# The first weight tile in halves around x, the first norm factors alone, and the compression sums in rows

## Chip, cores and metric
One core of one Trainium2 chip runs the kernel. The metric is the time on the device in microseconds, the median of the runs; all inputs and outputs are float32.

## The reference, cut to what matters
Two layers of a mixer over 512 positions of width 1024, and a final norm. Each layer norms x, multiplies by a wide `w_in`, feeds four branches (short convolution, sparse attention, retention, pooling), merges them and runs a gated feed-forward block. The part of the attention branch that the change touches compresses keys and values over overlapping windows of 32 positions, 16 apart (31 windows):

```python
def compress(t, w1, w2):
    tb = t[:, blk] + cmp_pe[None, None, :, None, :]     # blk: 31 windows of 32 positions
    hid = jax.nn.gelu(jnp.einsum('bnlgd,lde->bnge', tb, w1))
    return jnp.einsum('bnge,ef->bngf', hid, w2)

def hybrid_layer(x, norm1_g, w_in, ...):
    h = rms_norm(x, norm1_g)
    z = h @ w_in
...
```

## The kernel before
Activations lie transposed, features on the 128 partitions and the 512 positions along the free axis: x is eight blocks [128, 512]. Every weight matrix is cut into groups of 128x1024 (512 KB) of eight 128x128 chunks, which pass through a ring of three slots. Every product is made in three matmuls of a split: weights and activations are each kept as a high part (rounded by a copy) and a low part (the rest), and `product` (L1205 to L1207) adds high x high, high x low and low x high. So a tile of 512 columns costs 24 matmuls for its eight chunks, and two accumulator banks, `acc[0]` and `acc[1]`, take turns.

The engines' work is written out by hand, each engine in its own order, tied by counting semaphores. SyncE issues the weight groups: group g + 3 may come once the low half of group g is made. ScalarE makes the high parts (`w_hi`), VectorE the low parts of the first groups and of x, GpSimd all later low parts (L437). `hi_ready` and `lo_ready` count them, `lo_ready` twice for each group, because low parts are made in halves of four chunks, and TensorE waits for the second half only in the middle of a tile (`second_half`). The factors of all norms, gate biases, taps and the position terms `pe` lie in one table, `vc_` [128, 294] (147 KB), and `norm1` is its first eight columns.

At the start SyncE issues group 0, the table, the eight blocks of x, group 1, the square part of the constants, group 2, the other constants, group 3 and on. ScalarE makes w_hi of group 0 and then xg_hi block by block (L511), VectorE w_lo of group 0 and then xg_lo (L712), and TensorE follows a block behind (`wait=1` of tile 0). Until then TensorE runs 14 products of zeros (L1200). After that ScalarE makes group 1, two squares of x, group 2, six squares, and enters the loop over the layers, where each step first makes the high part two groups ahead. Tile 2 uses `acc[0]` again and so waits for ScalarE's copy of tile 0, k_cmp (L527).

The first twelve tiles of a layer (`A_TILES`) are the keys and values of the compression, the other keys and values, the queries and the gates. VectorE scales k_cmp and v_cmp by the norm and then adds the position terms (`windows`, L795): the 512 positions are split into even and odd (on the partitions, q), sixteen-position groups m (32 of them) and places r in them (8); the result `win` [128, 2, 2, 256] keeps, for each of two term sets a and each key group g, 32 x 8 values. After tile 6 TensorE multiplies them (`compress`, L1298): 16 steps l, each for k and v, of 31 windows for two key groups, 62 columns, with weights of 64 columns. k goes to the lower 64 output partitions, v to the upper ones. In VectorE's order `take` (L732) empties tiles: take(4), win_v, two rotations, take(5), a copy, take(6), and then the sums of the compression. Tile 7 goes to the bank that take(5) empties.

Of the kernel before, what the change touches and what calls it, by code (L numbers as in the profile page):

```python
# [23 lines left out]
F32 = mybir.dt.float32  # L24
F32R = mybir.dt.float32r
ALU = mybir.AluOpType
ACT = mybir.ActivationFunctionType
AX = mybir.AxisListType

P = 128  # L30
S = 512
D = 1024
DC = D // P
# [5 lines left out]
HEADS, KV_GROUPS, DH = 8, 2, 64  # L39
BLOCK, STRIDE = 32, 16  # L40
NCMP = (S - BLOCK) // STRIDE + 1
# [7 lines left out]
CH = 8  # L49
# [9 lines left out]
GROUPS = D0 + DC * DG  # L59
# [123 lines left out]
def build(nc, xT, weights, vec, w1, pool_w, consts, decay, out):  # L183
    with ExitStack() as ctx:
        sem = lambda name: ctx.enter_context(nc.semaphore(name))
# [5 lines left out]
        def at(name, shape, dt, offset):  # L191
            n = 4 * int(np.prod(shape[1:]))
            assert base + offset + n <= nc.sbuf_usable_end, (name, offset)
            return nc.alloc_sbuf_tensor_at(name, shape, dt, offset=base + offset)
# [4 lines left out]
        w_raw = at("w_raw", [P, RING, CH * P], F32, 48 * KB)  # L199
        w_hi = at("w_hi", [P, RING, CH * P], F32R, 60 * KB)  # L200
        w_lo = at("w_lo", [P, RING, CH * P], F32R, 72 * KB)
# [49 lines left out]
        vc_ = at("vec", [P, NVEC], F32, R3)  # L251
# [21 lines left out]
        def V(name, i=0, n=1):  # L273
            return vc_[:, VEC[name] + i:VEC[name] + i + n]
# [11 lines left out]
        raw_ready = [sem(f"raw_ready{i}") for i in range(RING)]  # L286
        hi_ready = sem("hi_ready")
        lo_ready = sem("lo_ready")
# [9 lines left out]
        mean_ready = sem("mean_ready")  # L298
        spread_ready = sem("spread_ready")
        vec_ready = sem("vec_ready")  # L300
        w2v_ready = sem("w2v_ready")
        w1_ready = [sem("w1k_ready"), sem("w1v_ready")]
        x_in = [sem(f"x_in{c}") for c in range(DC)]
# [77 lines left out]
        @block.sync  # L381
        def _(sp):
            def load_group(g, slot):
                sp.dma_start(w_raw[:, slot, :],
                             weights[bass.ds(g, 1), :, :].rearrange("a p n -> (a p) n")).then_inc(raw_ready[slot], 16)

            def load_groups(L, first, last):

                with sp.Fori(0, (last - first) // RING) as t:
                    for k in range(RING):  # L390
                        g = L * GROUPS + t * RING + (first + k)
                        sp.wait_ge(lo_ready, 1 + 2 * (g - (RING - 1)))
                        load_group(g + 0, (first + k) % RING)

            load_group(0, 0)
            sp.dma_start(vc_[:, :], vec[0, :, :]).then_inc(vec_ready, 16)
            for c in range(DC):
                sp.dma_start(x[:, c, :], xT[:, c, :]).then_inc(x_in[c], 16)
            load_group(1, 1)
            squares = CON["causal"]  # L400
            sp.dma_start(con[:, 0:squares], consts[:, 0:squares]).then_inc(square_ready, 16)
            load_group(2, 2)
            sp.dma_start(con[:, squares:], consts[:, squares:]).then_inc(con_ready, 16)
            with sp.Fori(0, LAYERS) as L:


                sp.wait_ge(halves, 1 + L * (2 * GROUPS))
                for k in range(RING):
                    g = RING + k
                    sp.wait_ge(lo_ready, 1 + 2 * (L * GROUPS + (g - (RING - 1))))  # L410
                    load_group(L * GROUPS + g, g % RING)
                    if k == 2:
                        sp.dma_start(w2v[DH:P, :], vec[bass.ds(L, 1), 0:DH, VEC["w2v"]:VEC["w2v"] + DH].rearrange("a p n -> (a p) n")).then_inc(w2v_ready, 16)
                    if k < 2:
                        sp.dma_start((w1k, w1v)[k][:, :, :],
                                     w1[bass.ds(L * 2 + k, 1), :, :, :].rearrange("a p l n -> (a p) l n")).then_inc(w1_ready[k], 16)
                load_groups(L, 2 * RING, D0 + RING)

                sp.wait_ge(act_ready, 1 + L * FC + FC)
                sp.dma_start(vc_[:, :], vec[bass.ds(L + 1, 1), :, :].rearrange("a p n -> (a p) n")).then_inc(vec_ready, 16)  # L420


                load_groups(L, D0 + RING, GROUPS + RING)
            for c in range(DC):
                sp.wait_ge(y_ready, c + 1)
                sp.dma_start(out[:, c, :], x[:, c, :]).then_inc(stored, 16)
            sp.wait_ge(stored, 16 * DC)
# [20 lines left out]
        def _(act):  # L448
# [47 lines left out]
                    act.dma_start(dst[64:128, :], src[0:64, :]).then_inc(rot_ready[i % 2], 16)  # L496


            act.wait_ge(zero_made, 2)
            nc.scalar.activation(pad_out, pad_out, ACT.Sqrt)  # L500

            def first_high(g):

                act.wait_ge(raw_ready[g], 16)
                nc.scalar.activation(w_hi[:, g, :], w_raw[:, g, :], ACT.Copy).then_inc(hi_ready, 1)

            first_high(0)
            act.wait_ge(vec_ready, 16)
            for c in range(DC):
                act.wait_ge(x_in[c], 16)  # L510
                nc.scalar.activation(xg_hi[:, c, :], x[:, c, :], ACT.Copy, scale=V("norm1", c)).then_inc(x_hi_ready, 1)  # L511
            first_high(1)
            for c in range(DC):
                if c == 2:
# [145 lines left out]
        def _(dve):  # L660
            ve = nc.vector
# [35 lines left out]
                dve.sem_inc(s, 1)  # L697
            ve.memset(rstd[:, 0:P], 0.0).then_inc(zero_made, 1)
            ve.memset(small[:, :], 0.0).then_inc(zero_made, 1)
            dve.wait_ge(vec_ready, 16)  # L700
            def first_low(g):

                dve.wait_ge(hi_ready, g + 1)
                for half in range(2):
                    part = slice(half * CH * P // 2, (half + 1) * CH * P // 2)
                    ve.tensor_tensor(w_lo[:, g, part], w_raw[:, g, part], w_hi[:, g, part].bitcast(F32),
                                     ALU.subtract).then_inc(lo_ready, 1)

            first_low(0)
            for c in range(DC):  # L710
                dve.wait_ge(x_hi_ready, c + 1)
                ve.scalar_tensor_tensor(out=xg_lo[:, c, :], in0=x[:, c, :], scalar=V("norm1", c), in1=xg_hi[:, c, :].bitcast(F32),  # L712
                                        op0=ALU.mult, op1=ALU.subtract).then_inc(xg_ready, 1)
# [11 lines left out]
            with dve.Fori(0, LAYERS) as L:  # L725
# [61 lines left out]
                def windows(src, dst, name):  # L787


                    view = src.rearrange("p (m r q) -> p q m r", r=STRIDE // 2, q=2)  # L790
                    pe_ = V("pe", 0, BLOCK).rearrange("p (a r q) -> p q a r", a=2, q=2)
                    for g in range(KV_GROUPS):
                        rows = slice(DH * g, DH * g + DH)
                        for q in range(2):
                            ins = ve.tensor_tensor(  # L795
                                dst[DH * q:DH * q + DH, :, g, :].rearrange("p a (m r) -> p a m r", r=STRIDE // 2),
                                view[rows, q, :, :].unsqueeze(1).to_broadcast([DH, 2, S // STRIDE, STRIDE // 2]),
                                pe_[rows, q, :, :].unsqueeze(2).to_broadcast([DH, 2, S // STRIDE, STRIDE // 2]), ALU.add)
                            if (g, q) != (1, 1):
                                ins.then_inc(chain, 1)  # L800
                                then.n += 1
                    v_end(ins, name)
# [364 lines left out]
                with dve.Fori(0, DC // 2) as t:  # L1167
# [3 lines left out]
                    for k in range(2):  # L1171
                        c = t * 2 + k
# [21 lines left out]
        def _(pe):  # L1194
# [1 line left out]
            used = {"s": 0, "t": 0}  # L1196
            pe.sem_inc(halves, 1)
            pe.wait_ge(zero_made, 1)
            for _ in range(14):
                mm(acc[1][:, 0:P], rstd[:, 0:P], rstd[:, 0:P], start=True, stop=True)  # L1200

            def product(tile, slot, chunk, right_hi, right_lo, first, last):
# [6 lines left out]
            with pe.Fori(0, LAYERS) as L:  # L1209
                used.update(s=0, t=0)  # L1210

                def group_here(g, loop=None, per=0):

                    v = L * GROUPS + (g + 1)
                    if loop is not None:
                        v = v + loop * per
                    pe.wait_ge(hi_ready, v)
                    pe.wait_ge(lo_ready, 2 * v)

                def second_half(g, loop=None, per=0):  # L1220

                    v = L * GROUPS + (g + 1)
                    if loop is not None:
                        v = v + loop * per
                    pe.wait_ge(lo_ready, 1 + 2 * v)

                def tile_free(T, loop=None, per=0):
# [57 lines left out]
                def window(win, l):  # L1285

                    a, r = l // (STRIDE // 2), l % (STRIDE // 2)
                    return win[:, a, :, :].rearrange("p g (m r) -> p g m r", r=STRIDE // 2)[:, :, a:a + NCMP, r]

                def compress():  # L1290
                    for kind, i in (("k", 0), ("v", 1)):
# [185 lines left out]
                for b in range(B_GROUPS):  # L1477
                    g = A_GROUPS + b
# [9 lines left out]
                with pe.Fori(0, DC) as j:  # L1488
# [4 lines left out]
                    for n in range(4):  # L1493
                        g = J0 + 4 + n // 2
# [13 lines left out]
                for j in range(DC):  # L1508
                    g, T = O0 + j, TO0 + j
# [25 lines left out]
                with pe.Fori(0, DC // 2) as t:  # L1535
                    for k in range(2):
                        tile_free(TD0 + k, t, 2)
                        for c in range(FC):
                            g = D0 + DG * k + c // CH
# [143 lines left out]
```

## Time and profile before

| | us |
|---|---|
| median of 3 runs | 2072.21 |
| lowest, highest | 2071.92, 2073.07 |
| the profiled execution: own time | 2073.4 |
| its span | 2071.6 |
| busy: TensorE | 2043.5 |
| busy: VectorE, GpSimd, ScalarE | 1197.5, 917.5, 685.5 |

The page and the trace are of one execution, and its times are microseconds from the span's start. A timeline row gives start, duration, engine, line and operation, output <- inputs, and in brackets the idle time before it and what ended it. A row of the chain gives start, duration and what the end hung on. PE is TensorE's matmul, DVE VectorE, ACT ScalarE, POOL GpSimd, SPq the issuing of transfers on SyncE. A float32 matmul stands as two records, one for each pass. PEclk is the granted clock as a share of full.

### The profile page before, as it was taken

What the parts mean: (1) busy time and instruction counts of PE and PEld (TensorE: products, weight loads), DVE (VectorE), ACT (ScalarE), POOL (GpSimd) and SP (SyncE); (2) the same over time, 40 slices, a digit from 0 to 9 for tenths busy, and PEclk for the clock granted to TensorE, in tenths of its full rate; (3) what the DMA queues carried; (4) which work ended last, traced back from release to release, by engine and by line L of the source; (5) the groups of instructions that cost most, each with busy time, mean ns of one, the idle gap of its engine ahead of it and who ended that gap; (6) DMA issues with size and microseconds to landing.
All of it is one profiled execution on the core that took longest, in us unless ns stands there. A gap on an engine that the chain in (4) does not pass through costs nothing.

```text
span 2071.6 us, 32027 instructions
## 1 busy us (share of the span) xinstructions
PE 2043.5 (99%) x9840; PEld 1639.5 (79%) x9840; DVE 1197.5 (58%) x1799; ACT 685.5 (33%) x1011; POOL 917.5 (44%) x672
## 2 busy tenths in 40 slices
PE   8999999999999999999999999999999999999997
PEld 7777677888888888888887777778888888888886
DVE  7766865422327788862258677572322378888522
ACT  5355533323332322222233554333323232222222
POOL 4432233544445554545544212334444445555552
PEclk9999999999999999999999999999999999999998
DMA  5311122232232223223233112222323223222333
GB/s 210 107 52 52 62 89 90 91 96 96 91 101 96 92 97 101 91 94 112 95 125 95 56 49 66 92 91 92 101 91 101 91 92 102 91 101 95 101 105 108
DMA packets 57433, 194.91 MB, mean 94 GB/s; under 512 B 7040, under 2 KB 7552, under 8 KB 57216
## 3 DMA queue, kind: packets, MB, share of 16 engines
q1 hardware_dynamic: 52576, 186.17, 26.9%
q10 hardware_dynamic: 4768, 7.61, 1.4%
q8 instruction: 50, 0.82, 0.2%
q14 instruction: 39, 0.32, 0.1%
HBM read 186.67 MB, written 2.10 MB: 91 GB/s over the span
## 4 chain that ended last, share of the span: by engine, by line
PE 95%; DVE 3%; issue 1%; ACT 0%; DMA 0%; SPq 0%; DVEq 0%; ACTq 0%
PE acc L1205 29%; PE acc L1207 28%; PE acc L1206 28%; PE o L1416 2%; PE s L1390 2%; PE t L1398 1%; PE o L1455 1%; PE s L1445 1%; PE t L1436 0%; PE s L1298 0%; DMA w_raw<-weights_dram 0%; PE s L1471 0%; PE s L1462 0%; DVE ssq L1104 0%; DVE x L1189 0%
## 5 line engine op out<-in xcount | busy, mean ns | idle before, releaser
L437 POOL TENSOR_TENSOR w_lo<-w_raw,w_hi 128x512 fp32r<-128x512 f32 x668 | 917.3, 1395 | 1130.1 <-ACT w_hi L459 1114.2
L1205 PE MATMUL acc<-xg_hi,w_hi 128*128 128x512 f32 x1904 | 768.8, 404 | 5.8 <-DVE xg_lo L712 1.8
L1207 PE MATMUL acc<-xg_hi,w_lo 128*128 128x512 f32 x1904 | 743.0, 390 | 0.0
L1206 PE MATMUL acc<-xg_lo,w_hi 128*128 128x512 f32 x1904 | 741.9, 390 | 0.0
L459 ACT ACTIVATE w_hi<-w_raw 128x1024 fp32r<-128x1024 f32 x336 | 355.0, 1056 | 772.3 <-PE acc L1207 737.4
L1205 PEld LDWEIGHTS acc<-xg_hi,w_hi 128*128 128x128 f32 x1904 | 357.5, 188 | 115.3 <-issue 29.5
L1206 PEld LDWEIGHTS acc<-xg_lo,w_hi 128*128 128x128 f32 x1904 | 357.8, 188 | 76.1 <-issue 5.8
L1207 PEld LDWEIGHTS acc<-xg_hi,w_lo 128*128 128x128 f32 x1904 | 357.4, 188 | 76.2
L1082 DVE TENSOR_TENSOR work<-acc,rstd 128x512 f32<-128x512 f32 x64 | 44.1, 690 | 256.1 <-PE acc L1207 256.1
L1205 PE MATMUL acc<-act_hi,w_hi 128*128 128x512 f32 x352 | 136.9, 389 | 0.0
L1206 PE MATMUL acc<-act_lo,w_hi 128*128 128x512 f32 x352 | 136.9, 389 | 0.0
L1207 PE MATMUL acc<-act_hi,w_lo 128*128 128x512 f32 x352 | 136.9, 389 | 0.0
L1088 DVE SCALAR_TENSOR_TENSOR work<-work,acc 128x512 f32<-128x512 f32 x64 | 44.0, 688 | 103.1 <-PE acc L1207 103.1
L1176 DVE SCALAR_TENSOR_TENSOR x<-acc,x 128x512 f32 x16 | 11.1, 693 | 158.1 <-PE acc L1207 158.1
L1205 PE MATMUL acc<-y_hi,w_hi 128*128 128x512 f32 x256 | 99.6, 389 | 0.0
L1206 PE MATMUL acc<-y_lo,w_hi 128*128 128x512 f32 x256 | 99.6, 389 | 0.0
L1207 PE MATMUL acc<-y_hi,w_lo 128*128 128x512 f32 x256 | 99.6, 389 | 0.0
L635 ACT ACTIVATE work<-work 128x512 f32<-128x512 f32 x44 | 27.8, 632 | 192.2 <-DVE work L1131 192.2
L940 DVE COPY pT<-t 128x128 f32<-128x128 f32 (+3 forms) x128 | 56.7, 484 | 56.3 <-PE o L1416 56.0
L1207 PEld LDWEIGHTS acc<-act_hi,w_lo 128*128 128x128 f32 x352 | 66.1, 188 | 13.8
L1205 PEld LDWEIGHTS acc<-act_hi,w_hi 128*128 128x128 f32 x352 | 66.1, 188 | 13.8
L1206 PEld LDWEIGHTS acc<-act_lo,w_hi 128*128 128x128 f32 x352 | 66.1, 188 | 13.6
(211 smaller groups left out, 2230.0 us busy)
## 6 DMA issues: line engine op xcount, KB each, us to landing
w_raw<-weights_dram SPq DMA_DIRECT2D x339, 512.0 KB, 3.3
x<-xT_dram SPq DMA_DIRECT2D x8, 256.0 KB, 5.9
rot<-rq ACTq DMA_DIRECT2D x16, 128.0 KB
rot<-rk ACTq DMA_DIRECT2D x16, 128.0 KB
dec<-decay_dram ACTq DMA_DIRECT2D x8, 256.0 KB, 3.2
out_dram<-x SPq DMA_DIRECT2D x8, 256.0 KB, 2.7
con<-consts_dram SPq DMA_DIRECT2D x1, 1406.0 KB, 10.5
w1k<-w_dram SPq DMA_DIRECT2D x2, 512.0 KB, 8.9
```

The costliest lines, as they stand in the source:

```text
L437: nc.gpsimd.tensor_tensor(w_lo[:, slot, part], w_raw[:, slot, part], w_hi[:, slot, part].bitcast(F32), ALU.subtract).then_inc(lo_ready, 1)
L459: nc.scalar.activation(w_hi[:, slot, :], w_raw[:, slot, :], ACT.Copy).then_inc(hi_ready, 1)
L635: nc.scalar.activation(work[:, 2, :], work[:, 1, :], ACT.Tanh, scale=0.5).then_inc(silu_ready, 1)
L940: t_end(ve.tensor_copy(pT[:, u % 2, 0:w], t_of(e)[:, 0:w]), e)
L1082: ve.tensor_tensor(work[:, n, :], acc[n % 2][:, :], rstd[:, :], ALU.mult).then_inc(acc_free, 1)
L1088: ve.scalar_tensor_tensor(out=work[:, n, :], in0=work[:, n, :], scalar=1.0, in1=acc[n % 2][:, :], op0=ALU.add, op1=ALU.mult).then_inc(acc_ ...
L1205: mm(tile, w_h, right_hi, start=first, stop=False)
L1206: mm(tile, w_h, right_lo, start=False, stop=False)
L1207: return mm(tile, w_l, right_hi, start=False, stop=last)
L1390: mm(b[:, 0:w], qT[r, h % 4, qi * P:(qi + 1) * P], kT[r, br, 0:w], start=True, stop=True).then_inc(s_done, 1)
L1398: ins = nc.tensor.transpose(b[:, k * P:(k + 1) * P], pr_of(u)[:, k * P:(k + 1) * P], ident)
L1416: ins = mm(o_bank[qi % 2][d, j * P:(j + 1) * P], v[:, d], p[:, half, :], start=(br == 0 and k == 0), stop=(br == 1 and k == qi + 1))
```

## The change
The first weight group is loaded in two halves: the first ahead of x, the second between blocks 1 and 2 of x, and ScalarE and VectorE make its high and low parts in the same two halves. The eight columns of `norm1` are loaded alone, on ScalarE's queue; the rest of the table comes behind group 1. TensorE waits for the second half of w_hi in the middle of tile 0. The zero products go from 14 to 9. And `win` is stored with r outside and m inside, so that VectorE writes with a step of 32 elements and TensorE reads 31 neighbours for each key group.

```diff
@@ SyncE
-            load_group(0, 0)
-            sp.dma_start(vc_[:, :], vec[0, :, :]).then_inc(vec_ready, 16)
+            middle = CH * P // 2
+            sp.dma_start(w_raw[:, 0, 0:middle], weights[0, :, 0:middle]).then_inc(first_raw, 16)
             for c in range(DC):
                 sp.dma_start(x[:, c, :], xT[:, c, :]).then_inc(x_in[c], 16)
+                if c == 1:
+                    sp.dma_start(w_raw[:, 0, middle:], weights[0, :, middle:]).then_inc(raw_ready[0], 16)
             load_group(1, 1)
+            sp.dma_start(vc_[:, DC:], vec[0, :, DC:]).then_inc(vec_ready, 16)
@@ ScalarE
+            act.dma_start(vc_[:, 0:DC], vec[0, :, 0:DC]).then_inc(gain_ready, 16)
             act.wait_ge(zero_made, 2)
...
-            first_high(0)
-            act.wait_ge(vec_ready, 16)
+            act.wait_ge(first_raw, 16)
+            nc.scalar.activation(w_hi[:, 0, 0:middle], w_raw[:, 0, 0:middle], ACT.Copy).then_inc(first_hi, 1)
+            act.wait_ge(gain_ready, 16)
             for c in range(DC):
                 act.wait_ge(x_in[c], 16)
                 nc.scalar.activation(xg_hi[:, c, :], x[:, c, :], ACT.Copy, scale=V("norm1", c)).then_inc(x_hi_ready, 1)
+                if c == 1:
+                    act.wait_ge(raw_ready[0], 16)
+                    nc.scalar.activation(w_hi[:, 0, middle:], w_raw[:, 0, middle:], ACT.Copy).then_inc(hi_ready, 1)
@@ VectorE
-            dve.wait_ge(vec_ready, 16)
+            dve.wait_ge(gain_ready, 16)
...
-            first_low(0)
+            dve.wait_ge(first_hi, 1)
+            ve.tensor_tensor(w_lo[:, 0, 0:middle], w_raw[:, 0, 0:middle], w_hi[:, 0, 0:middle].bitcast(F32), ALU.subtract).then_inc(lo_ready, 1)
             for c in range(DC):
+                if c == 2:
+                    dve.wait_ge(hi_ready, 1)
+                    ve.tensor_tensor(w_lo[:, 0, middle:], w_raw[:, 0, middle:], w_hi[:, 0, middle:].bitcast(F32), ALU.subtract).then_inc(lo_ready, 1)
                 dve.wait_ge(x_hi_ready, c + 1)
@@ VectorE, windows
-                                dst[DH * q:DH * q + DH, :, g, :].rearrange("p a (m r) -> p a m r", r=STRIDE // 2),
+                                dst[DH * q:DH * q + DH, :, g, :].rearrange("p a (r m) -> p a m r", r=STRIDE // 2),
@@ TensorE
-            for _ in range(14):
+            for _ in range(9):
                 mm(acc[1][:, 0:P], rstd[:, 0:P], rstd[:, 0:P], start=True, stop=True)
...
+                    if g == 0 and loop is None:
+                        pe.wait_ge(first_hi, 1)
+                        pe.wait_ge(lo_ready, 2 * (L * GROUPS + 1))
+                        return
...
+                    if g == 0 and loop is None:
+                        pe.wait_ge(hi_ready, v)
                     pe.wait_ge(lo_ready, 1 + 2 * v)
...
-                    return win[:, a, :, :].rearrange("p g (m r) -> p g m r", r=STRIDE // 2)[:, :, a:a + NCMP, r]
+                    return win[:, a, :, :].rearrange("p g (r m) -> p g r m", r=STRIDE // 2)[:, :, r, a:a + NCMP]
```

## Rows read from the trace of the kernel before

**Rows 1.** The page's part 4, shares of the chain by engine.
```profile
PE 95%; DVE 3%; issue 1%; ACT 0%; DMA 0%; SPq 0%; DVEq 0%; ACTq 0%
```

**Rows 2.** Timeline of the head, ScalarE and TensorE.
```profile
6.83 5.49 ACT L511 ACTIVATE xg_hi<-x,vec 128x512 fp32r<-128x512 f32 x8 [1.62 <-DMA x<-xT_dram]
...
8.39 0.50 PE L1205 MATMUL acc<-xg_hi,w_hi 128*128 128x512 f32 x1 [1.76 <-DVE xg_lo L712]
...
19.23 1.28 ACT L459 ACT_TABLE_LOAD   x1
...
22.21 0.47 PE L1205 MATMUL acc<-xg_hi,w_hi 128*128 128x512 f32 x1 [1.57 <-ACT k_cmp L527]
```

**Rows 3.** Chain of waits in the head: start, duration, what.
```profile
5.68 7.34 DMA w_raw<-weights_dram
...
15.05 1.03 ACT w_hi L505
16.08 3.13 ACT first_sq L516 x6
```

**Rows 4.** Chain of waits, small products: squares, compression, vc, values.
```profile
27.91 0.79 PE s L1274 x8
...
51.57 3.80 PE s L1298 x64
...
67.19 0.36 PE s L1337 x16
...
179.34 1.02 PE o L1416 x16
...
226.39 1.24 PE o L1416 x20
```

**Rows 5.** Instructions of two lines: duration in ns, min/median/max.
```profile
L1298 PE MATMUL s<-win_k,w1k x64: 292/294/305, 51.5 to 1077.8; 128*64 128x62 f32 x64
...
L1416 PE MATMUL o<-pT,v_nat x8: 272/273/323, 158.2 to 158.5; 128*64 128x128 f32 x8
```

**Rows 6.** Timeline around the compression, layer 0 and layer 1.
```profile
41.71 4.92 DVE L795 TENSOR_TENSOR win_v<-v_cmp,vec 64x512 f32<-64x512 f32 x4
...
52.73 0.68 DVE L732 TENSOR_TENSOR sc<-acc,rstd 128x512 f32<-128x512 f32 x1
...
55.30 0.50 PE L1205 MATMUL acc<-xg_hi,w_hi 128*128 128x512 f32 x1
...
61.10 0.69 DVE L732 TENSOR_TENSOR qT<-acc,rstd 128x512 f32<-128x512 f32 x1 [4.41 <-PE acc L1207]
...
1075.32 0.68 DVE L732 TENSOR_TENSOR sc<-acc,rstd 128x512 f32<-128x512 f32 x1
...
1078.02 0.50 PE L1205 MATMUL acc<-xg_hi,w_hi 128*128 128x512 f32 x1
```

**Rows 7.** Instructions of line 795 that write win_k, both layers.
```profile
L795 DVE TENSOR_TENSOR win_k<-k_cmp,vec x8: 739/749/755, 33.5 to 1058.6; 64x512 f32<-64x512 f32 x8
```

**Rows 8.** Issues of x, groups 2 and 3 (timeline), their landing times (last column).
```profile
1.68 3.96 SPq L398 DMA_DIRECT2D x<-xT_dram  x8
...
7.06 0.64 SPq L384 DMA_DIRECT2D w_raw<-weights_dram  x1
...
8.76 0.35 SPq L384 DMA_DIRECT2D w_raw<-weights_dram  x1
...
x<-xT_dram SPq DMA_DIRECT2D x1, 256.0 KB, 5.1
...
w_raw<-weights_dram SPq DMA_DIRECT2D x1, 512.0 KB, 7.7
...
w_raw<-weights_dram SPq DMA_DIRECT2D x1, 512.0 KB, 10.7
```

**Rows 9.** TensorE in two stretches: us, busy (records), granted clock, DMA share, GB/s.
```profile
1.71:4.91 3.20, 3.20 (x15) 1.00 0.92 278
4.91:6.63 1.72, 1.72 (x15) 1.00 0.91 292
```

More of the change, by code:

```diff
@@ L300, in build @@
         vec_ready = sem("vec_ready")
+        gain_ready = sem("gain_ready")
+        first_raw = sem("first_raw")
+        first_hi = sem("first_hi")
         w2v_ready = sem("w2v_ready")
@@ L505, in first_high @@
                 nc.scalar.activation(w_hi[:, g, :], w_raw[:, g, :], ACT.Copy).then_inc(hi_ready, 1)
-            first_high(0)
-            act.wait_ge(vec_ready, 16)
+            middle = CH * P // 2
+            act.wait_ge(first_raw, 16)
+            nc.scalar.activation(w_hi[:, 0, 0:middle], w_raw[:, 0, 0:middle], ACT.Copy).then_inc(first_hi, 1)
+            act.wait_ge(gain_ready, 16)
             for c in range(DC):
@@ L707, in first_low @@
                                      ALU.subtract).then_inc(lo_ready, 1)
-            first_low(0)
+            middle = CH * P // 2
+            dve.wait_ge(first_hi, 1)
+            ve.tensor_tensor(w_lo[:, 0, 0:middle], w_raw[:, 0, 0:middle], w_hi[:, 0, 0:middle].bitcast(F32), ALU.subtract).then_inc(lo_ready, 1)
             for c in range(DC):
+                if c == 2:
+                    dve.wait_ge(hi_ready, 1)
+                    ve.tensor_tensor(w_lo[:, 0, middle:], w_raw[:, 0, middle:], w_hi[:, 0, middle:].bitcast(F32), ALU.subtract).then_inc(lo_ready, 1)
                 dve.wait_ge(x_hi_ready, c + 1)
```

## The prediction
> **What bounds the kernel now.** I read the page first. The chain that ended last runs 95% over TensorE's matmuls [rows 1]. So a microsecond is only worth something where TensorE itself does less, or where it stands still and what it waits for comes sooner. The change touches two such places: the first 22 us, and the block of compression products (L1298), which stands once in each layer.
>
> For the head I followed the chain of waits backwards from where TensorE last stands still. Tile 0 of the projections begins at 8.39, after 1.76 us of waiting for xg_lo; but TensorE stands again before tile 2, 1.57 us until 22.21, for the ScalarE copy of k_cmp [rows 2]. Everything gained before 22.21 that doesn't move that copy is given back there. The chain to it is ScalarE's: group 1 lands at 13.02, its high half follows, group 2's high half starts at 15.05, six squares end at 19.21, a table load of 1.28 us, w_hi, k_cmp [rows 2, 3]. The reader is to see that ScalarE, not TensorE, is the clock of the first 22 us.
>
> For the compression products: 64 records take 3.80 us in the chain. k and v go to different halves of the columns and start together, so this is 32 rounds of 0.119 us with the edges, for 62 columns [rows 4]. The values products load weights of the same shape (128x64, two halves) and stream 128 columns: their runs of 16 and 20 records take 1.02 and 1.24 us, so two rounds cost 0.22, one 0.11, or 0.86 ns a column. At that rate 62 columns are 0.053 us. That the rounds here take twice this, and that one matmul of 62 columns lasts 294 ns where one of 128 lasts 273 [rows 5], needs a reason. The visible difference is the moving operand: L1298 reads with a step of 8 elements (32 bytes), the values products read neighbours.
>
> **The change, part by part.** *Rows instead of interleaved sums.* L795 writes win as (r m) instead of (m r), and L1298 reads runs of 31 neighbours. Counts and shapes stay. If the step is the reason, a round falls from about 0.115 to 0.055: 32 x 0.060 = 1.9 us less in each layer. Two things could hold it up. Weight loads: eight records with 128-wide loads and one moving column take 0.79 us, 0.1 each [rows 4]; two 64-wide loads one after the other would also be 0.1, and nothing would be won. Against that stand the vc products, 16 records with 31-wide loads in 0.36 us, where loads in series would need 16 x 0.024 = 0.39 before any edge [rows 4]; and the values rounds hide both loads. So loads into different column halves overlap, and I take 0.055 to 0.06 a round; the bounds are 0.055 and no gain.
>
> What is late next: tile 7 needs acc[1], which VectorE frees with take(5). That ends at 53.41 while tile 7 starts at 55.30; in layer 1 at 1076.00 against 1078.02 [rows 6]. So at most 1.89 and 2.02 us can be taken, less a few hundredths for the signal. The gain just fits under this cap. take(7) follows a VectorE pause of 4.41 us [rows 6], so VectorE can follow from there on. I take 1.75 us a layer, 3.5 for both.
>
> VectorE's side: win_k's instructions last 749 ns each [rows 7], win_v's four in layer 0 take 4.92 us [rows 6] while GpSimd works on weights; an ordinary 512-column one lasts 0.68 to 0.69 [rows 6]. The write step goes from 4 to 128 bytes; the trace has no VectorE write with such a step. Lower bound nothing: the engine takes about 1.4 ns an element here, against TensorE's 0.86 a column, so it has more time for each access. Upper bound: what TensorE pays for its step. A matmul of 62 neighbours should last 273 less 66 columns of 0.86, 216 ns; 294 is 78 more, 1.3 ns a column. On 512 elements that is 0.65 us an instruction, 5.2 us for eight. It is nearest to L795 itself, whose reads already step over every second element and cost 0.06 us more than ordinary; I take 0 to 0.1 us for the eight together. If it is more, take(5) comes later by that much and every bit over the slack lands on tile 7. win_v is written at 41.71 + 4.92 = 46.63 [rows 6] and L1298 begins at 51.57 [rows 4], so the products themselves wait for it hardly even at the upper bound.
>
> *The head.* Before x0 SyncE now issues half of group 0 (256 KB) instead of all of it and the vector table (512 + 147 KB). x0 was issued at 1.68 and landed 5.1 later, at 6.78 [rows 8]; from there to group 1's landing at 13.02 [rows 3] came seven blocks and a group, 2304 KB, 370 KB/us. With 403 KB less ahead of it x0 comes up to 1.09 us sooner, near 5.7, and tile 0 begins near 7.3. But the second half of group 0 now stands between x1 and x2, so x2 to x7 gain only the table's 147 KB, 0.40 us. On ScalarE the second half of w_hi goes between x1 and x2 as well. ScalarE took 5.49 us for eight blocks [rows 2]; it has the lead of x0 to fit 0.6 us in. VectorE's w_lo of that half fits the same way. Group 1 is issued at the same place in SyncE's list (ten DMAs before it both times) and lands 0.40 sooner, 12.62. Group 2 now has the rest of the table ahead of it: the same bytes before it as before, so it lands at 7.06 + 7.7 = 14.76 as it did [rows 8], and its high half can't start before 14.8 instead of 15.05. So only 0.24 us of the head gets through: squares to 18.97, table load to 20.3, and group 3, landed at 8.76 + 10.7 = 19.46 [rows 8], doesn't stop w_hi. The moved part of the table and the constants behind it are issued some 0.5 us later; the cover is the full queue (7 to 10 us from issue to landing [rows 8]), and the table's first reader, VectorE's half_b, stands behind the eight sums of squares. The new small DMA (eight floats a partition) goes out on ScalarE's queue ahead of the table load; one of SyncE's issues takes 0.5 us (3.96 for eight [rows 8]), its landing has some three microseconds until x0's, and ScalarE would stand idle for w_raw anyway. If an issue there took longer than that idle time, only tile 0 would see it. Bounds for the head: 0.4 if group 2 lands earlier too, and 0.3 more if the queue starts more evenly; on the other side the 128 small packets and the later issues could take back the 0.24 and 0.2 more. I take 0.24.
>
> *Nine warm-up products for fourteen.* Records come at 0.213 us in the first 3.20 us (15 of them) and at 0.115 in the next 1.72 (15), while the granted clock column says 1.00 in both [rows 9]: TensorE goes from the pace of 1.2 GHz to that of 2.4 at 4.9. 18 records end near 5.3, long before x0; five products taken off cost nothing on the path. What they do to the clock is a rival.
>
> Sum: 3.5 + 0.24 = 3.74. The profiled execution had a span of 2071.6 and its own time 2073.4, 1.8 around the span that the change doesn't touch: 2067.9 and 2069.7. That execution stood 1.2 above the median 2072.21, so I forecast 2068.5. A measurement of this kernel can tell about 0.2%, 4.1 us, from no change: the forecast is a real gain that lies just inside.
>
> **The rivals.**
> *VectorE pays for the scattered writes* (other side). Place: the eight L795. With S the extra time of a layer's eight, tile 7 waits for take(5), so it starts S - 1.95 later than before (the mean slack of the two layers), whatever the products save. The kernel is slower by over 0.2% from 2(S - 1.95) - 0.24 = 4.1 on, S = 4.1, 0.5 us an instruction. At the upper bound, S = 5.2, it is 2 x 3.25 - 0.24 = 6.3 slower: 2078.5. For it: TensorE's rate for a step. Against: VectorE needs over 1.3 ns an element anyway. By the Trainium skill (SBUF — State Buffer, the section on the DMA port swizzle) SBUF has lines of 16 bytes, and each access that goes on to a new line pays: that would make TensorE's reads cheap and every write of L795 dear. By that rule this case is the likelier; the trace agrees for the read, and has no row for the write. Chance 0.07.
> *A small write price*, 0.1 to 0.3 us each, S = 0.8 to 2.4: take(5) becomes the limit and a layer gains 1.95 - S, 1.15 to -0.45: with the head 2069.7 to 2072.9. Chance 0.17.
> *The compression products don't get faster* (loads or issue bound them): only the head, 2072.0. Chance 0.13.
> *The clock stays low*: 18 warm-up records end within half a microsecond of the rise, and a pause of 2 us follows. If tile 0 starts at 1.2 GHz, three microseconds of products at half pace cost 1.6; TensorE has 1.57 + 0.24 of idle time before tile 2, so it is hidden and the time is the forecast's. It costs only if it lasts into tile 2. Chance of a visible loss 0.03: about 2070.
> *Forecast*: 0.60, own range 2067.4 to 2069.4; about four tenths of it lies under 2068.07, if the head gives more.
>
> **Numbers.** Faster by over 0.2%: 0.27, from the forecast alone. Slower: 0.07 and a little of the small price, 0.08. Within: 0.65. The range 2067.3 to 2072.2 takes in the forecast, the small price and the case without gain.
>
> **What would show it.** In the profile after: the L1298 chain piece near 1.9 us instead of 3.80, its matmuls near 215 ns; L795 still near 749; tile 7 of layer 0 near 53.5 and started by TensorE's own order or by VectorE's take; xg_hi at 5.8; group 1's high half at 12.7, group 2's at 14.8; tile 2 at 22.0. Wrong would be: L795 over 0.85 us, a TensorE wait for VectorE before tile 7, a round that stays over 0.1, or a tile 2 that starts at 22.2 or later.

## The result, and the profile after

The changed kernel takes 2081.49 us (median of 6 runs, 2079.61 to 2083.28), the kernel before 2072.8 beside it (6 runs, 2071.92 to 2073.07). The ratio is 1.0044, with a 95% interval of 1.0033 to 1.0056: the change makes the kernel slower, by 8.7 us. The prediction said 2068.5 with a range up to 2072.2, and gave 0.08 to slower: it was wrong, and its first rival was right in place and sign.

The page of the kernel after, its span and the chain that ended last by engine (line numbers of the kernel after are 17 to 23 higher around here: L795 is now L812, L732 is L749, L1205 is L1222, L1298 is L1321):

```profile
span 2079.6 us, 32010 instructions
...
PE 93%; DVE 5%; issue 1%; ACT 0%; DMA 0%; DVEq 0%; SPq 0%; ACTq 0%
```

VectorE's part of the chain has grown from 3% [rows 1] to 5%. Where it sits the instructions of the two changed lines show, with minimum, median and maximum in ns; they answer to [rows 5, 7]:

```profile
L812 DVE TENSOR_TENSOR win_k<-k_cmp,vec x8: 1099/1109/1992, 34.3 to 1064.4; 64x512 f32<-64x512 f32 x8
L812 DVE TENSOR_TENSOR win_v<-v_cmp,vec x8: 1095/1119/1289, 44.9 to 1075.1; 64x512 f32<-64x512 f32 x8
...
L1321 PE MATMUL s<-win_k,w1k x64: 222/222/268, 52.3 to 1080.8; 128*64 128x62 f32 x64
```

Both sides of the bet are here. TensorE's matmul of 62 columns falls from 294 to 222 ns, as forecast. VectorE's sum goes from 749 to some 1100 ns, which was forecast to cost nearly nothing. TensorE's list of waits has this as its first row (total, times, longest):

```profile
PE acc L1222 <- DVE sc L749: 9.6, 4, 4.2
```

Before, two such waits held 1.5 us together. The new ones stand in front of tile 7, once in each layer. VectorE's timeline of that stretch in layer 0 (start, us, line, operation):

```profile
33.60 0.69 DVE L848 TENSOR_TENSOR k_cmp<-k_cmp,rstd 128x512 f32<-128x512 f32 x1 [2.02 <-DVEq L786]
34.32 5.40 DVE L812 TENSOR_TENSOR win_k<-k_cmp,vec 64x512 f32<-64x512 f32 x4
...
44.86 4.73 DVE L812 TENSOR_TENSOR win_v<-v_cmp,vec 64x512 f32<-64x512 f32 x4
49.63 0.69 DVE L794 TENSOR_TENSOR rot<-rot,con 128x512 f32<-128x512 f32 x1
50.24 1.78 DVE L796 TENSOR_TENSOR kT<-kT,con 128x512 f32<-128x512 f32 x1
52.05 1.66 DVE L798 TENSOR_TENSOR kT<-kT,rot 128x512 f32<-128x512 f32 x1
53.63 1.77 DVE L794 TENSOR_TENSOR rot<-rot,con 128x512 f32<-128x512 f32 x1
55.33 1.74 DVE L796 TENSOR_TENSOR kT<-kT,con 128x512 f32<-128x512 f32 x1
57.11 0.69 DVE L798 TENSOR_TENSOR kT<-kT,rot 128x512 f32<-128x512 f32 x1
57.72 0.68 DVE L749 TENSOR_TENSOR sc<-acc,rstd 128x512 f32<-128x512 f32 x1
```

take(5) is the last row. It starts at 57.72 and not at 52.73 [rows 6], 4.99 later, of which 0.79 came in with the head (win_k starts at 34.32, [rows 6, 7] put it at 33.5). The other 4.2 us arise in this stretch: win_k 5.40 instead of four of 0.75 with their gaps, 2.3 longer, and the rotations 2.0 longer, though nothing in them was changed: four of the six take 1.7 us instead of 0.69, where before it were two. Those of 1.7 us run beside GpSimd's subtractions. GpSimd's timeline of the same time, after:

```profile
49.83 3.33 POOL L443 TENSOR_TENSOR w_lo<-w_raw,w_hi 128x512 fp32r<-128x512 f32 x2 [4.67 <-ACT w_hi L465]
53.59 2.94 POOL L443 TENSOR_TENSOR w_lo<-w_raw,w_hi 128x512 fp32r<-128x512 f32 x2 [0.43 <-ACT w_hi L465]
```

and before, where the two rotations that started inside the first of these rows (48.62 and 50.30) took 1.76 and 1.78:

```profile
48.02 3.52 POOL L437 TENSOR_TENSOR w_lo<-w_raw,w_hi 128x512 fp32r<-128x512 f32 x2 [3.57 <-ACT w_hi L459]
52.82 2.53 POOL L437 TENSOR_TENSOR w_lo<-w_raw,w_hi 128x512 fp32r<-128x512 f32 x2 [1.28 <-ACT w_hi L459]
```

On TensorE's side, the timeline and the stretches (busy us and count of PE, PEld, DVE, ACT and POOL, then PEclk, DMA share, GB/s):

```profile
58.55 0.70 PE L1222 MATMUL acc<-xg_hi,w_hi 128*128 128x512 f32 x1 [4.20 <-DVE sc L749]
```

```profile
54.00:58.50 4.50, 0.36 (x13) 0.22 (x8) 4.37 (x4) 0.00 (x0) 2.53 (x2) 1.00 0.54 168
58.50:60.00 1.50, 1.45 (x4) 1.19 (x5) 1.44 (x3) 0.00 (x0) 0.00 (x0) 0.54 0.48 194
60.00:62.00 2.00, 2.00 (x6) 1.55 (x5) 0.93 (x5) 0.00 (x0) 0.00 (x0) 0.50 0.08 14
62.00:64.00 2.00, 2.00 (x10) 1.63 (x9) 0.00 (x0) 1.33 (x2) 0.00 (x0) 0.99 0.10 18
```

TensorE ends the compression at 54.35 and stands until 58.55. Then the granted clock is 0.54 and 0.50, 1.2 GHz, until 62. The chain of waits shows what that costs:

```profile
59.68 0.43 PE acc L1224
60.10 0.43 PE acc L1222
...
62.44 0.23 PE acc L1222
```

A matmul takes 0.43 us of the chain and later 0.23. The nine that start from 58.55 on need 3.7 us, where nine at full clock need 2.1: another 1.6 us. Layer 1 repeats all of it: the stretch is 4.07 longer there (take(5) from 1075.32 to 1084.07, with win_k starting 4.68 later), TensorE waits 3.90, and behind the wait some four matmuls still start 0.23 to 0.30 apart, then eight 0.43 apart: the clock takes 1.6 us again.

The head, on ScalarE's timeline, against [rows 2, 3]:

```profile
3.58 0.63 ACT L516 ACTIVATE w_hi<-w_raw 128x512 fp32r<-128x512 f32 x1 [0.89 <-DMA w_raw<-weights_dram]
5.14 0.72 ACT L520 ACTIVATE xg_hi<-x,vec 128x512 fp32r<-128x512 f32 x1 [0.94 <-DMA x<-xT_dram]
...
13.60 1.06 ACT L512 ACTIVATE w_hi<-w_raw 128x1024 fp32r<-128x1024 f32 x1 [0.61 <-DMA w_raw<-weights_dram]
...
15.81 1.06 ACT L512 ACTIVATE w_hi<-w_raw 128x1024 fp32r<-128x1024 f32 x1
...
22.27 0.58 ACT L539 ACTIVATE k_cmp<-acc 128x512 f32<-128x512 f32 x1
```

ScalarE begins the first block 1.7 us sooner, but group 1 is 0.56 later, group 2's high half 0.76 later, and tile 2 starts at 22.99 instead of 22.21. The span by stages: tile 2 +0.8, cmp_keys of layer 0 (86.06 to 90.87) +4.8, end of layer 0 (677.41 to 682.45) +5.0, end +8.0.

### The profile page after: what moved, and what is told of

Its sections match the earlier page's. It is cut to its first block, busy times and chain, and to the rows that moved or that the text cites. A ratio compares the mean times of both kernels' runs of the same rounds, so it can differ in the third digit from the quotient of the medians.

```text
span 2079.6 us, 32010 instructions
## 1 busy us (share of the span) xinstructions
PE 2045.4 (98%) x9830; PEld 1639.0 (79%) x9830; DVE 1202.0 (58%) x1799; ACT 686.0 (33%) x1012; POOL 919.4 (44%) x672
## 4 chain that ended last, share of the span: by engine, by line
PE 93%; DVE 5%; issue 1%; ACT 0%; DMA 0%; DVEq 0%; SPq 0%; ACTq 0%
PE acc L1222 28%; PE acc L1224 28%; PE acc L1223 28%; PE o L1439 2%; PE s L1413 2%; PE t L1421 1%; PE o L1478 1%; PE s L1468 1%; PE t L1459 0%; DVE win_k L812 0%; PE s L1494 0%; PE s L1485 0%; DVE sc L749 0%; DVE kT L796 0%; DMA w_raw<-weights_dram 0%
## 5 line engine op out<-in xcount | busy, mean ns | idle before, releaser
L1222 PE MATMUL acc<-xg_hi,w_hi 128*128 128x512 f32 x1904 | 771.5, 405 | 11.8 <-DVE sc L749 9.6
L1222 PEld LDWEIGHTS acc<-xg_hi,w_hi 128*128 128x128 f32 x1904 | 358.9, 189 | 122.1 <-issue 36.6
L1222 PE MATMUL acc<-act_hi,w_hi 128*128 128x512 f32 x352 | 136.9, 389 | 0.0
L1222 PE MATMUL acc<-y_hi,w_hi 128*128 128x512 f32 x256 | 99.6, 389 | 0.0
L1222 PEld LDWEIGHTS acc<-act_hi,w_hi 128*128 128x128 f32 x352 | 66.1, 188 | 13.8
```

Of the source, the lines that this page charges most:

```text
L1222: mm(tile, w_h, right_hi, start=first, stop=False)
```

## Experiments

The theory is that the layout costs the time through VectorE: its writes with a step of 128 bytes make take(5) late, and TensorE's pause for it costs the clock as well. The rivals are the head, the products, and other causes of VectorE's lateness; each expectation names its own theories. All ratios are against the kernel before on the same chip, with 95% intervals; the edits are against the kernel before unless said otherwise.

**The layout alone.**

```
-   dst[...].rearrange("p a (m r) -> p a m r", r=STRIDE // 2),
+   dst[...].rearrange("p a (r m) -> p a m r", r=STRIDE // 2),
...
-   return win[...].rearrange("p g (m r) -> p g m r", r=STRIDE // 2)[:, :, a:a + NCMP, r]
+   return win[...].rearrange("p g (r m) -> p g r m", r=STRIDE // 2)[:, :, r, a:a + NCMP]
```

> Only the layout of win is changed (VectorE writes with a step of 128 bytes, TensorE reads neighbours); the head is that of before. Theory (late take): VectorE's window sums of 1.1 instead of 0.75 us put take(5) some 4 us later, TensorE waits about 4 us before tile 7 in each layer and runs at half pace for some 3 us behind the wait. The head's part was +0.8, so this gives 2072.8 + 7.2 = 2080, with L1298 at 1.96 us. Rival (the head and its transfers are the cause): 2069 to 2070, no long wait before tile 7.

Measured: 2083.13 us (2081.29 to 2083.67), ratio 1.0049 (1.0035 to 1.0063). Its waits of TensorE:

```profile
PE acc L1205 <- DVE sc L732: 9.6, 4, 4.2
```

The same row as in the kernel after. The whole loss is in the layout.

**The head alone** (all of the change but those two lines).

> Only the head is changed (halves of group 0, norm1 alone, nine warm-up products); win is laid out as before. Theory: tile 2 starts 0.8 us later, as in the changed kernel's profile, nothing else: 2073.6. Rival (the head is the cause): about 2080. My forecast for the head, 0.24 faster, would give 2072.6.

Measured: 2073.27 (2072.48 to 2075.03), ratio 1.0003 (0.9994 to 1.0012). The time can't be told from the kernel before; k_cmp starts at 22.13 in its trace, against 21.48 before. But over the ten traces of this study with the head of before it runs from 21.48 to 22.23, with a median of 21.78, and over the three with the new head from 21.89 to 22.27, with a median of 22.13. The trace of before was the earliest of its ten, and only some 0.35 us can be the head's.

**The read alone, and the write alone.** The first has only the second pair of lines above, the second only the first pair; both leave the sums in another order than their reader takes them.

> TensorE reads win as rows, VectorE still writes it interleaved as before, so the compression is computed from wrongly ordered sums; the work of both engines is otherwise that of before. Theory (the step of 32 bytes is what slowed the reads, VectorE's write step is what costs): 1.84 us less in each layer with take(5) just in time, 2069.2. Rival (the shorter products are no gain on the path, or need the new write): 2072.8.

> VectorE writes win as rows, TensorE reads it by the old step of 32 bytes, so the compression is computed from wrongly ordered sums; the work of both engines is otherwise the same. The products take 3.80 us again, so TensorE pauses about 2.3 us before tile 7 instead of 4.2. Theory: take(5) sets tile 7's start, the same as with the layout alone; if the shorter pause leaves the clock up, 2078, which would make the shorter products not only useless but the cause of the fall of the clock; if the clock falls all the same, 2081 to 2083. Rival (VectorE's price comes from both engines using rows at once, not from the write): VectorE back at 0.75 us a sum and 2072.8.

Measured: the read alone 2069.49 (2068.61 to 2070.13), ratio 0.9984 (0.9975 to 0.9993); the write alone 2079.75 (2078.93 to 2083.08), ratio 1.0038 (1.0024 to 1.0052). From the chain of the first, and one line's instructions:

```profile
51.88 2.01 PE s L1298 x64
```

```profile
L795 DVE TENSOR_TENSOR win_k<-k_cmp,vec x8: 737/750/759, 33.9 to 1056.7; 64x512 f32<-64x512 f32 x8
```

The second's:

```profile
L795 DVE TENSOR_TENSOR win_k<-k_cmp,vec x8: 1099/1110/1993, 34.3 to 1062.6; 64x512 f32<-64x512 f32 x8
```

```profile
PE acc L1205 <- DVE sc L732: 5.9, 4, 2.2
```

So the forecast's gain exists: 3.80 us of products become 2.01, twice, and 3.4 us come off the time with nothing lost. And the writes alone, with the products as slow as before, cost 6.9. Together they don't add to 3.5 but to 10.2 with the layout alone. The products that end 1.8 us sooner gain nothing there, since tile 7 waits for VectorE; they only lengthen TensorE's pause, from 2.2 to 4.2 us. In the write alone's trace the clock stays at full after layer 0's pause of 2.2 us, and falls after layer 1's.

**The layout with nine filler products behind the compression**, which keep TensorE busy until take(5) is nearly there.

```
+   for _ in range(9):
+       mm(o_bank[0][0:DH, 0:256], w1k[:, 0, :], win_k[:, 0, 0, :], start=True, stop=True)
```

> The layout alone, and behind the compression products nine more float32 products of 256 columns (3.9 us, into a bank that nobody reads then) that keep TensorE busy while VectorE comes to take(5). They change no result. Tile 7 starts as late as before the addition. Theory (part of the loss is the clock, which falls in the pause): the granted clock stays 1.00 and only the delay of tile 7 is left, 2.5 us a layer: 2078. Rival (the half pace behind tile 7's start has another reason): 2081 to 2083 as with the layout alone.

Measured: 2078.34 (2077.39 to 2078.92), ratio 1.0026 (1.0016 to 1.0035). Its stretches:

```profile
54.00:58.00 4.00, 3.71 (x18) 2.07 (x17) 3.85 (x4) 0.00 (x0) 2.01 (x2) 1.00 0.52 179
58.00:60.00 2.00, 1.97 (x9) 1.67 (x10) 1.90 (x5) 0.00 (x0) 0.00 (x0) 1.00 0.37 139
```

Tile 7 starts at 58.03, as late as with the layout alone (58.09), yet at full clock, and the kernel is 4.8 us shorter (3.9 between the two spans). Work that computes nothing makes it faster. The rows say the same: in the trace of the layout alone the slow matmuls cost 1.6 us behind layer 0's pause and 2.6 behind layer 1's, against the same tiles here. So the clock's share is shown: some 4 to 5 us of the 10 with the layout alone, 3.2 in the trace of the kernel after.

**take(5) ahead of the rotations**, in the kernel after, and with the layout alone.

```
                 windows(v_cmp[:, :], win_v, "win_v")
+                take(5, sc[:, 1, :])
...
-                take(5, sc[:, 1, :])
```

> The changed kernel with one line moved: VectorE does take(5) right behind win_v, before the two rotations, so that tile 7's bank is free about 7 us sooner. Theory: no wait before tile 7, no fall of the clock, and the whole 1.85 us of the shorter products in each layer counts: 2072.8 + 0.8 - 3.7 = 2070. Rival (slow window sums hold something else up too, so the wait only moves to a later tile): 2076 or more.

> The layout alone with take(5) moved ahead of the two rotations. The slow scattered sums stay. Theory: 3.6 us faster than before, 2069.2, TensorE's next wait for VectorE is the one before tile 12 as always. Rival (the sums delay more than take(5)): 2073 or more.

Measured: 2071.26 (2070.64 to 2074.74), ratio 0.9996 (0.9987 to 1.0005), and 2071.97 (2070.98 to 2073.11), ratio 0.9996 (0.9987 to 1.0005). One moved line takes back the 10 us of the kernel after:

```profile
49.25 0.69 DVE L749 TENSOR_TENSOR sc<-acc,rstd 128x512 f32<-128x512 f32 x1
```

take(5) is done before the compression ends at 54, and only the two old waits of 0.8 are left of that row. But the full gain of 3.4 doesn't come: with the layout alone it is 0.9. A new wait shows in both traces, 0.8 us in the first, and in the second:

```profile
PE s L1344 <- DVE kc L855: 1.3, 1, 1.3
```

VectorE is as late as before; it only owes its time to someone else. Against the read alone, TensorE gets past these products (L1344) 1.65 us later in layer 0 and 0.43 in layer 1: that is 2.1 of the 2.5 us that are missing.

**Neighbours in the write, a step of 64 bytes in VectorE's read.**

```
-   view = src.rearrange("p (m r q) -> p q m r", r=STRIDE // 2, q=2)
+   view = src.rearrange("p (m r q) -> p q r m", r=STRIDE // 2, q=2)
...
```

The output and the position terms are walked in the same new order, and TensorE reads neighbours.

> The same rows in win, made the other way round: VectorE goes through r outside and m inside, so that it writes neighbours and reads k_cmp and v_cmp with a step of 64 bytes. Theory A (only the scattered write costs): sums of 0.75 us, take(5) in time, 2069.3, faster than before. Theory B (every access to a new 16-byte line costs, read or write): 1.1 us or more and 2081 to 2083.

Measured: 2075.38 (2073.22 to 2077.1), ratio 1.0011 (1.0002 to 1.002).

```profile
L795 DVE TENSOR_TENSOR win_k<-k_cmp,vec x8: 1021/1038/1898, 33.8 to 1061.5; 64x512 f32<-64x512 f32 x8
```

1038 ns against 1109: VectorE pays for a read with a step too. The time fits neither theory of the run, 2.5 us above before: take(5) starts at 55.19, earlier than the 57.26 of the layout alone, and TensorE pauses 2.13 and 2.16 us instead of 4.20 and 3.90. The clock falls behind both pauses.

**The order changed once, in the products before.** k and v are multiplied by rstd in one instruction each, ahead of the eight sums. These two write their result in rows (sc[:, 2] and sc[:, 3]), and the sums read and write neighbours.

```
+   def to_rows(dst, src):
+       old = lambda t: t.rearrange("p (m r q) -> p m r q", r=STRIDE // 2, q=2)
+       return ve.tensor_tensor(dst.rearrange("p (q r m) -> p m r q", q=2, r=STRIDE // 2),
+                               old(src), old(rstd[:, :]), ALU.mult)
...
+   then(to_rows(sc[:, 2, :], k_cmp[:, :]))
+   windows(sc[:, 2, :], win_k, "win_k")
...
```

> The head of before. The rows are made once, in VectorE's two products by rstd (L831, L833), which now write k_cmp and v_cmp sorted by parity, place and group into free buffers; the eight window sums then read and write neighbours. Theory (a price per scattered instruction of about 0.35 us, paid twice instead of eight times): products of 1.0 to 1.1 us, sums back under 0.75, take(5) at most 0.4 us later than before, no pause over 0.3 us before tile 7, 2069.6. Rival (512 scattered elements on 128 partitions cost more, or the sums are slow for their four-dimensional pattern and not for the step): sums stay at 1.0 or more and 2075 to 2080.

> The same with take(5) ahead of the two rotations. Theory: nothing is left to wait for before tile 7 and VectorE is not behind later either: 2069.2, within 0.5 us of the one without the move. Rival (as with rows_take5, the work behind take(5) comes too late for a later tile): 2071.

Measured: 2069.18 (2068.44 to 2070.12), and with take(5) early as well 2069.16 (2067.83 to 2069.91); ratio 0.9984 (0.9975 to 0.9993) for both. This beats both kernels, by 3.3 and 12 us.

```profile
L799 DVE TENSOR_TENSOR win_k<-sc,vec x8: 682/686/1793, 34.5 to 1057.2; 64x512 f32<-64x512 f32 x8
```

```profile
33.38 1.09 DVE L789 TENSOR_TENSOR sc<-k_cmp,rstd 128x512 f32<-128x512 f32 x1 [2.02 <-DVEq L769]
...
53.26 0.68 DVE L732 TENSOR_TENSOR sc<-acc,rstd 128x512 f32<-128x512 f32 x1
```

Two instructions pay the 0.4 us of scattered writes instead of eight, and the eight fall from 749 to 686. The stretch from the first product to take(5) is as long as before (53.26 - 33.38 = 19.88, and 52.73 - 32.81 = 19.92), so take(5) fits into the slack, and the early take(5) has nothing left to win. Against these 686 ns the read with a step of 64 bytes costs 352 ns, and against 749 the write with a step of 128 bytes 360: VectorE pays about the same at either end.

**GpSimd's work cut short, with the layout alone.** What doubles the rotations? Rotations of over 1 us overlap GpSimd's subtractions in every trace (30 to 114 and 1050 to 1122 us). Here GpSimd subtracts 32 of every 512 columns; the low parts of the others stay stale, so the sums are not the reference's.

> The kernel before with the change of layout alone, as in the run with the layout alone, but GpSimd subtracts only 32 of the 512 columns in each half of a weight group (all groups but the first of its groups), so the low parts of the other columns are stale and the sums are not the reference's. The question is where the 4.2 us come from by which VectorE's take(5) is late. Theory A: only some 1.4 us of them are the scattered writes before win_k's end; the rest is that VectorE, once late, runs its instructions with two operands in SBUF beside GpSimd, where each takes 1.7 us and not 0.69 (six of ten in the run with the layout alone). Then every win_k and win_v instruction takes 1.10 us, every rotation 0.69, the stretch from the first win_k to take(5) shrinks from 23.4 us to 16 or 17, TensorE doesn't wait before tile 7, and the time is 2069 to 2070 or lower. Theory B: the double durations come from something else (transfers, TensorE's reads): the rotations still take 1.7 us, the wait of 4 us before tile 7 stays, and the time is 2080 to 2083. If both, the wait shrinks to 1 or 2 us, and the time is 2072 to 2076.

Measured: 2059.31 (2059.08 to 2059.55), ratio 0.9936 (0.9918 to 0.9953). No wait before tile 7.

```profile
L795 DVE TENSOR_TENSOR win_k<-k_cmp,vec x8: 1100/1116/1158, 34.0 to 1053.5; 64x512 f32<-64x512 f32 x8
```

```profile
33.98 4.57 DVE L795 TENSOR_TENSOR win_k<-k_cmp,vec 64x512 f32<-64x512 f32 x4
...
47.48 0.68 DVE L779 TENSOR_TENSOR kT<-kT,con 128x512 f32<-128x512 f32 x1
48.19 0.69 DVE L781 TENSOR_TENSOR kT<-kT,rot 128x512 f32<-128x512 f32 x1
48.80 0.74 DVE L777 TENSOR_TENSOR rot<-rot,con 128x512 f32<-128x512 f32 x1
49.47 0.74 DVE L779 TENSOR_TENSOR kT<-kT,con 128x512 f32<-128x512 f32 x1
...
50.85 0.68 DVE L732 TENSOR_TENSOR sc<-acc,rstd 128x512 f32<-128x512 f32 x1
```

Theory A of this run holds: no sum above 1.16, no rotation above 0.74, and the stretch from win_k to take(5) takes 16.87 us instead of 23.41 (57.26 - 33.85 in the layout alone). Its time was missed: 10 us more came off than expected. Waits elsewhere shrink too: TensorE's for cmp_pT from 4.0 to 0.8, and its weight loads, which with the layout alone waited for GpSimd's low parts 20 times, 10.7 us in all, never do here. So the 13 us aren't all VectorE's meetings with GpSimd, and the run doesn't split them. By subtraction it gives the split of the 4.2: eight writes cost 8 x 0.35 = 2.8 themselves. Without them the stretch would be 14.1 here, and it was 19.19 before, so 5.1 us of meetings with GpSimd stood in it before and 6.5 do with the layout alone: the remaining 1.4.

**The table moved, group 0 whole, fourteen warm-up products**: of the head's parts only the norm's factors alone and the rest of the table behind group 1.

> Of the head only the table: norm1 loaded alone on ScalarE's queue, the rest behind group 1; group 0 whole, fourteen warm-up products, win as before. Theory (what took the 0.24 us back was the split of group 0 and the early start of the slow transfers of x): tile 2 no later than before, 2072.6 to 2072.9. Rival (the 128 packets of 32 bytes or the later table did it): the k_cmp copy 0.4 us or more later than in before and 2073.3.

Measured: 2071.93 (2071.23 to 2075.15), ratio 0.9999 (0.999 to 1.0008).

```profile
12.52 1.06 ACT L507 ACTIVATE w_hi<-w_raw 128x1024 fp32r<-128x1024 f32 x1 [0.57 <-DMA w_raw<-weights_dram]
```

```profile
21.92 0.47 PE L1207 MATMUL acc<-xg_hi,w_hi 128*128 128x512 f32 x1 [1.82 <-ACT k_cmp L529]
```

Tile 2 starts 0.29 sooner than before, where the forecast of the head said 0.24, and k_cmp (21.19) sooner than in any of the ten traces with the head of before. With the split as well it came at 21.89 to 22.27. So the split in halves, or the five products taken off with it, seems to take back what the table gives, and somewhat more; but this is one trace against three, and the times are too coarse to show it.

## Why the prediction was wrong

- **TensorE's products: right.** 64 records take 2.01 us instead of 3.80, 222 ns each (forecast: 1.9, near 215). The two weight loads overlap, and the read alone took 3.4 us off the time; the forecast said 3.5.
- **VectorE's write price: the step that failed.** "I take 0 to 0.1 us for the eight together". It is 0.35 us each, 2.8 for the eight. The bounds, nothing and 5.2, held it. By the rival's formula this price alone makes the kernel 2 x (2.8 - 1.95) - 0.24 = 1.5 us slower; the rest of the 8.7 is in the items below. The choice between them went by the wrong nearness: L795's own reads with every second element said little about a step of 128 bytes, and "it has more time for each access" was a reason without a row. The one row with a large step in it, TensorE's 294 against 273 ns [rows 5], was kept as the far end, though it was the only evidence.
- **The rule that spoke against the change.** The runs agree with it on both sides: the reads got cheap, and the writes dear. It stood in the prediction with the words "By that rule this case is the likelier", at a chance of 0.07. By the Trainium skill (SBUF — State Buffer, the section on the DMA port swizzle) every access that goes on to a new line of 16 bytes pays; here that is 72 ns for 62 columns on TensorE (294 against 222) and about 350 ns for 512 elements on VectorE. None of these sums and products has a step between 8 and 32 bytes, so the runs don't show where the price begins.
- **What the lateness meets.** The rival priced S as eight writes and nothing more, and wanted 0.5 us from each for S = 4.1. S was 4.2 and 4.07 with only 0.35 from each, so that it met the rival's number is luck: 2.8 of writes, and 1.4 because later instructions meet more of GpSimd's work. Rows for it were in the prediction: win_v's four at 4.92 "while GpSimd works on weights", against 3.0 for four of 749. It read them as a level, not as something that moves with the time at which an instruction starts.
- **The rival's sum.** With S = 4.14 its formula gives 2 x (4.14 - 1.95) - 0.24 = 4.1 slower, just where the rival draws its line. The span grew by 8.0. The missing 3.9 are the clock, 2 x 1.6, and the head, 0.8 later in place of 0.24 sooner, 1.0 together: 8.3 (of the 0.8 about half is scatter, as the head alone showed). Forecast and rival had the clock only as a matter of the head; that a pause in front of tile 7 is charged a second time, in half-speed matmuls, was in neither.
- **The slack: right, and what made it decisive.** 1.9 us stood between take(5) and tile 7, and that slack took the first 1.9 of S.
- **The head: the sign failed, the size is small.** x0 5.14 and tile 0 6.70 (forecast 5.7 and 7.3): the front came even sooner. Then "lands 0.40 sooner, 12.62" failed for group 1: issued at 5.76, nearly as before, it landed at 13.56, 7.8 us later. And group 2, of which it said "it lands at 7.06 + 7.7 = 14.76 as it did", landed at 15.8 (7.79 + 8.0), since SyncE issues it 0.73 later behind one more transfer. Only the table's part alone gained, 0.29 in its one trace. That a gain ahead of tile 2 is given back was right. That fewer warm-up products cost nothing was right too: in the head alone the granted clock was 0.77 between 8 and 13 us, and TensorE still had 1.15 us to wait before tile 2.
- **Two small slips.** About four tenths of 0.60 are 0.24, not the 0.27 given to faster; and the range to 2072.2 doesn't take in the small price as a whole, which reached 2072.9.

What stays open: how the split in halves makes groups 1 and 2 later, whether by the one transfer more in SyncE's list or by the slower start of the reads of x; and whether three traces at 21.89 to 22.27 against nine around 21.78 are a loss in time at all.

## What to carry to other kernels

A layout has two ends: price the writer's step with the same row as the reader's, and then put the change of order where it is written once (here two products of rstd instead of eight sums). If a change makes an engine late that feeds the bound one, list what its next instructions will meet at their new times, and what the clock does after the pause; here these two doubled a cost of 2.8 us a layer. Before shortening work ahead of a wait, move what the wait is for: with take(5) first, the same change was no loss.

## What the runs showed of the hardware

- VectorE, fp32 sums of 64x512: 686 ns with neighbours on both sides, 749 with the order of before (reads of every second element), 1038 with a read step of 64 bytes, 1109 with a write step of 128 bytes.
- TensorE, 62 columns: 294 ns with a step of 32 bytes, 222 with neighbours; a round of two took 0.119 and takes 0.06.
- A VectorE instruction with its operands in SBUF takes 1.7 us instead of 0.69 beside GpSimd's subtraction (the rotations), one that writes with a step up to 1.99. With GpSimd's work cut to a sixteenth no rotation took over 0.75 and no sum over 1.16, VectorE's busy time fell from 1203.0 to 943.0 us, and the kernel took 13 us less than before.
- After pauses of 3.9 and 4.2 us in busy work TensorE's granted clock went to 0.50 for 3 to 5 us. Of four pauses of 2.1 to 2.3 us it stayed at full after one (layer 0 of the write alone) and fell after three (layer 1 of the write alone, both layers of the read with a step).
